# Turning round the column order of every product with weights in a two-layer fp32 encoder

## What is computed

```python
def reference(x, mem, ...):
    h = x
    for l in range(DEPTH):                      # DEPTH = 2
        h = h + hybrid_mixer(rms_norm(h, mix_norm_g[l]), w_in[l], ..., w_out[l])
        h = h + memory_cross_attention(rms_norm(h, xattn_norm_g[l]),
                                       rms_norm(mem, mem_norm_g[l]),
                                       w_xq[l], w_xk[l], w_xv[l], w_xo[l])
        h = h + conv_ffn(rms_norm(h, ffn_norm_g[l]), w_up[l], ffn_conv_w[l],
                         ffn_conv_b[l], w_down[l])
    return rms_norm(h, final_norm_g)
```

## Time and profile before

| | |
|---|---|
| median of 3 runs | 904.4 us (902.22 to 905.19) |
| profiled execution, its own time | 903.87 us |
| span, first to last instruction | 902.0 us |
| mean granted TensorE clock | 0.992 |
| TensorE busy | 879.2 us, 97% |
| VectorE, ScalarE busy | 627.5 and 525.9 us, 70% and 58% |
| moved | 146.7 MB at 163 GB/s |

### The profile page before, as it was taken

One profiled execution on the slowest core, in us unless ns is written; L12 is line 12 of the kernel. 1 busy time (PEld: TensorE's weight loads), 2 busy tenths in 40 slices (PEclk: granted clock), 3 DMA queues, 4 the chain that ended last, 5 costly groups with the idle time before them and its releaser, 6 DMA issues.

```text
span 902.0 us, 13410 instructions
## 1 busy us (share of the span) xinstructions
PE 879.2 (97%) x5452; PEld 774.5 (86%) x5452; DVE 627.5 (70%) x914; ACT 525.9 (58%) x782; POOL 12.9 (1%) x37
## 2 busy tenths in 40 slices
PE   6999999999999999999999999899999899999997
PEld 6999998788888888888899999888888788888885
DVE  5788487858557767667676875877664677667665
ACT  6864573557547556555667546636646555556555
POOL 5000000000000000000000000000000000000000
PEclk9999999999999999999999999999999999999999
DMA  9735543455154655565558254335362356555541
GB/s 284 220 98 158 168 152 131 141 186 187 47 187 155 218 190 184 187 191 183 140 170 225 63 166 159 140 96 187 109 217 94 108 176 230 187 190 184 187 164 47
DMA packets 128679, 146.68 MB, mean 163 GB/s; under 512 B 23164, under 2 KB 109546, under 8 KB 128618
## 3 DMA queue, kind: packets, MB, share of 16 engines
q1 hardware_dynamic: 128404, 145.55, 49.8%
q10 hardware_dynamic: 214, 0.28, 0.1%
HBM read 144.77 MB, written 1.05 MB: 162 GB/s over the span
## 4 chain that ended last, share of the span: by engine, by line
PE 90%; DVE 5%; ACT 4%; issue 1%; DMA 0%; DVEq 0%; ACTq 0%
PE bank L718 21%; PE bank L680 15%; PE bank L682 14%; PE bank L681 14%; PE bank L719 11%; PE bank L753 2%; DVE wlo L1446 2%; PE bank L851 2%; ACT whi L1100 2%; PE bank L1022 2%; PE bank L1009 2%; PE bank L772 1%; PE bank L883 1%; PE bank L893 1%; PE bank L860 1%; PE bank L976 1%
## 5 line engine op out<-in xcount | busy, mean ns | idle before, releaser
L1446 DVE TENSOR_TENSOR wlo<-raw,whi 128x2048 fp32r<-128x2048 f32 (+3 forms) x144 | 306.5, 2134 | 104.9 <-ACT whi L1100 104.4
L718 PE MATMUL bank<-ypair,whi 128*128 128x512 f32 x832 | 294.9, 398 | 0.6 <-DVE ypair L1462 0.5
L1100 ACT ACTIVATE whi<-raw 128x2048 fp32r<-128x2048 f32 (+3 forms) x144 | 256.4, 1786 | 39.5 <-PE bank L682 32.1
L719 PE MATMUL bank<-ypair,wlo 128*128 128x256 f32 x832 | 233.5, 281 | 0.0
L718 PEld LDWEIGHTS bank<-ypair,whi 128*128 128x128 f32 x832 | 156.2, 188 | 40.3 <-DVE wlo L1446 1.4
L719 PEld LDWEIGHTS bank<-ypair,wlo 128*128 128x128 f32 x832 | 157.1, 189 | 0.8
L680 PE MATMUL bank<-xhi,whi 128*128 128x256 f32 x320 | 94.9, 297 | 1.9 <-DVE wlo L1446 1.2
L681 PE MATMUL bank<-xlo,whi 128*128 128x256 f32 x320 | 92.4, 289 | 0.0
L682 PE MATMUL bank<-xhi,wlo 128*128 128x256 f32 x320 | 92.2, 288 | 0.0
L680 PE MATMUL bank<-whi,xhi 128*128 128x512 f32 (+2 forms) x256 | 90.0, 352 | 0.0
L682 PE MATMUL bank<-whi,xlo 128*128 128x512 f32 (+2 forms) x256 | 88.5, 346 | 0.0
(11 more groups left out here) (259 smaller groups left out, 1192.7 us busy)
## 6 DMA issues: line engine op xcount, KB each, us to landing
raw<-in_w_up SPq DMA_DIRECT2D x44, 1024.0 KB, 5.0
raw<-in_w_down SPq DMA_DIRECT2D x22, 1024.0 KB, 4.9
raw<-in_w_in SPq DMA_DIRECT2D x10, 1024.0 KB, 6.1
raw<-in_w_xk SPq DMA_DIRECT2D x8, 1024.0 KB, 4.8
raw<-in_w_xv SPq DMA_DIRECT2D x8, 1024.0 KB, 5.0
raw<-in_w_out SPq DMA_DIRECT2D x8, 1024.0 KB, 5.0
raw<-in_w_xq SPq DMA_DIRECT2D x8, 1024.0 KB, 4.7
raw<-in_w_xo SPq DMA_DIRECT2D x8, 1024.0 KB, 4.9
```

The source lines that it names most:

```text
L718: mm(o, hi[:, k, cs], ypair[:, k].rearrange("p a n -> p (a n)"), start=k == 0, stop=False, skip_group_check=True)
L719: last = mm(o[:, 0:T], lo[:, k, cs], yhi[:, k, :], start=False, stop=k == KT - 1, skip_group_check=True)
L1100: A(whi[:, gu % RING, 0:SIZE[gu]], raw[:, gu % RING, 0:SIZE[gu]], ACT.Copy).then_inc(hi_done, 1)
L1446: tt(wlo[:, gu % RING, 0:n_], raw[:, gu % RING, 0:n_], whi[:, gu % RING, 0:n_], ALU.subtract).then_inc(lo_done, 1)
```

## The change

A new helper `falling` issues every product with weights. It puts `[:, ::-1]` on the output and on the moving operand, so that column n of the output is still the product with moving column n, but the last column goes first. The stationary operand, the counts, the flags and the semaphores stay. For the 512-column product of `fm_joint` the order is that of hi and lo together: the lo half from its last column, then the hi half. The instructions on every engine stand in the same sequence before and after; in the changed kernel all products with weights carry the line of the helper, 681.

```diff
--- before.py
+++ after.py
@@ -676,10 +676,14 @@
                 def have(key):
                     pe.wait_ge(lo_done, UNIT[key] + 1)
 
+                def falling(o, s, m, first, last):
+
+                    return mm(o[:, ::-1], s, m[:, ::-1], start=first, stop=last, skip_group_check=True)
+
                 def split_mm(o, s_hi, s_lo, m_hi, m_lo, first, last):
-                    mm(o, s_hi, m_hi, start=first, stop=False, skip_group_check=True)
-                    mm(o, s_hi, m_lo, start=False, stop=False, skip_group_check=True)
-                    return mm(o, s_lo, m_hi, start=False, stop=last, skip_group_check=True)
+                    falling(o, s_hi, m_hi, first, False)
+                    falling(o, s_hi, m_lo, False, False)
+                    return falling(o, s_lo, m_hi, False, last)
 
                 def weights(key, nk):
                     gu = UNIT[key]
@@ -715,8 +719,8 @@
                             if fresh and f == 0:
                                 lo_is(pe, l, "n2" if name[:2] == "xq" else "n3", k)
                             cs = slice(f * P, f * P + P)
-                            mm(o, hi[:, k, cs], ypair[:, k].rearrange("p a n -> p (a n)"), start=k == 0, stop=False, skip_group_check=True)
-                            last = mm(o[:, 0:T], lo[:, k, cs], yhi[:, k, :], start=False, stop=k == KT - 1, skip_group_check=True)
+                            falling(o, hi[:, k, cs], ypair[:, k].rearrange("p a n -> p (a n)"), k == 0, False)
+                            last = falling(o[:, 0:T], lo[:, k, cs], yhi[:, k, :], False, k == KT - 1)
                         last.then_inc(te_done, 1)
 
                 def fm_unit(name, group, fresh=False):
@@ -750,8 +754,7 @@
                             lo_is(pe, l, group, k)
                         for i, (x, w) in enumerate(((xh, hi), (xh, lo), (xl, hi))):
                             for t in range(TT):
-                                last = mm(bank(names[t])[:, 0:n], x[:, k, t * P:(t + 1) * P], w[:, k, :],
-                                          start=k + i == 0, stop=False, skip_group_check=True)
+                                last = falling(bank(names[t])[:, 0:n], x[:, k, t * P:(t + 1) * P], w[:, k, :], k + i == 0, False)
                     last.then_inc(te_done, 1)
 
                 def tm_unit(unit, names, n, group, fresh=False):
```

## The result

The changed kernel takes 908.7 us in the median of 5 runs (908.19 to 910.38) against 904.4 before (902.22 to 905.19). The ratio is 1.0054, with a 95% interval from 1.0041 to 1.0068: slower by 4.9 us (3.7 to 6.1). The forecast was 904 and no change, with 901 to 907 around it; 908.7 lies outside that, but inside the wide range of 861 to 960, in which both a gain and a loss had a place.

What follows compares the result with a forecast made beforehand. TensorE, busy 97% of the span, was taken to set the end. The profiled 903.87 us + 1,640,448 columns x 0 + 4304 products x 0 gave 903.9, forecast as 904 us, own range 901 to 907, wide range 861 to 960.

Steps and rivals of the forecast that it cites:

- What bounds the kernel: Whole span: TensorE, busy 97%, sets the end; an added nanosecond per product is added to the time in full.
- No instruction moves, the waits stay, the distance between two writes of a column: All engines: counts, flags and waits unchanged; in the joint pair's bank the rewrite distances swap order, costing nothing new.
- The write with a step of minus one: Output of products with weights to PSUM, written backwards: taken as nothing per column, bounded with the read at 0.413 ns.
- The read with that step: Moving operand of products with weights, read backwards from SBUF: taken as nothing per column, slow end 0.413 ns more.
- 4304 x 0: Fixed part of all 4304 products with weights: no change, bounded by 10 ns less and 13 ns more each.
- the zero for each column: The 1,640,448 columns of products with weights: 0 ns more each, as every row with a backward step shows none.
- The prediction's own sign of being wrong: Distances between TensorE starts, 227 ns at 512 columns and 120 at 256: forecast wrong if either moves over 1 ns.
- The nearest rows: VectorE scans, 680 ns either way, and ScalarE and VectorE PSUM reads: a step of minus one is free there.
- Half pace: Rival at every column of products with weights: 0.413 ns more each, + 678 us, 1582 us in all; chance 0.18.
- The start price per product: Rival on 4304 products: a backward pattern costs 0 to 13 ns once each, 0 to 56 us; chance 0.10.
- A smaller fixed part: Rival on 4304 products: the 13 ns shrink to 3 ns, 43 us less, 861 us; chance 0.05.
- the prediction's second reading: Skill's PSUM line rule read as two accesses in a row must share a line: the backward step is free.

Runs made afterwards that it cites:

- The stream kernel: Not the encoder: 32 products a line from one stationary and one moving buffer, no other engine at work; falling against rising, bf16 216 and 216 ns at 512 columns.

## Why the prediction was wrong

**What bounds the kernel** held. TensorE has no cover, and the 5.2 us of the distances are 4.9 in the result. One reading was off: the first 45 us and the last 12 hold 14.8 of TensorE's 22.8 idle us, not all; another 5.9 lie between 560 and 735 us, a window that the rows did not show. They did not matter here.

**No instruction moves, the waits stay, the distance between two writes of a column**: nothing in the runs contradicts them beyond small things. TensorE's wait for `wlo` grew from 1.2 to 2.6 us, and its first wait shrank from 9.5 to 9.0. The joint pair's 353.2 ns fall only 0.4 behind.

**The write with a step of minus one**, taken as free: right, 0.9995.

**The read with that step**: here the sum failed. I had split a product into 0.418 ns a column and a fixed 13 ns from two distances, and taken both as constants of the engine, the second with the reason that the same stationary load stands between the products. The fixed part is not fixed. With a falling read it is 12 ns at 256 columns and 20 at 512. With a rising one it changes with the size of the stationary load (with half of it, from 13 to 7 ns at 256 columns and from 13 to 17 at 512) and with what ran before: the same rising down projection at 227.1 and 229.3 ns, the same joint pair at 346.9 and 352.8. The term that was 4304 x 0 should have been 1104 x 4 to 6.4 ns, 192 x 4 ns and 1056 x -1.7 ns, or 1.2 ns a product in the mean: 5.2 us. Split as the prediction did it, the falling distances would give 0.449 ns a column and 3.5 ns fixed, so the zero for each column failed with it; but that split misses the widths between (175.9 ns for 384 columns, where 177.8 were measured). The prediction's own sign of being wrong, a distance that moves by more than 1 ns, was met at both widths.

**The nearest rows**, scans and PSUM reads backwards on VectorE and ScalarE, were the wrong witnesses. I had written that they have a slower stream and drew the value from them all the same. The stream kernel shows the limit: TensorE itself is as indifferent as they are with bf16 and plain float32.

**The rivals.** Half pace did not happen: at 512 columns 438 ns were named and 233 came. The start price per product (chance 0.10, 0 to 56 us) had the sign and the size in its range, but the wrong law; it was to be the same at 256 and at 512 columns, and it is a loss at one and a gain at the other. A smaller fixed part (0.05) came true for 256 columns alone.

**The rule on lines** in the Trainium skill, page "SBUF — State Buffer", section "Door 1: The DMA port swizzle", sets the limit for SBUF at 16-byte lines and names PSUM as the place where a pattern costs. For PSUM the runs bear out the prediction's second reading, by which a fall is free: turned round it costs nothing (0.9995). For SBUF the rule does not give what was measured: blocks of 4 float32r columns that fall, each as long as a line and read in full, cost as much as a plain fall (233.4 ns), while a fall inside blocks of 4 costs nothing (226.6).

**Still open**: by what the read's order, the stationary load and the preceding stream set the 227, 229 or 233 ns of a product; what puts the pairs on the faster pace where nothing falls; and where the gain of the 256-column products goes.

## What to carry to other kernels

Where TensorE sets the end, measure the distance between starts, not the duration, and for each width: a change of half a per cent can be the sum of a loss at one width and a gain at another. An effect of a few nanoseconds a product need not add up over parts of a change, since a stream's pace can depend on what entered it; here three turned products ahead of each 32 pairs saved 3.8 us, nearly as much as the whole change had cost. Take the price of a new access from the engine and the data type that will make it, or keep the range open.

## What the runs showed of the hardware that was not expected

- With 128 stationary columns a float32r product reads its moving columns in order at 227 ns for 512 and 120 for 256; from last to first at 233 and 118; bf16 takes 216 at 512 in both directions. With 64 stationary columns it is 230 and 114 in order, 233 and 118 backwards. Writing PSUM backwards is free (0.9995).
- Blocks of 16 columns that rise, read backwards inside, cost 266.6 ns at 512 columns, 18% more than in order; blocks of 64 falling cost 227.5.
- A repeated pair of a 512- and a 256-column product has two steady paces, 352.8 and 346.9 ns, and keeps the one it entered for 32 pairs. Falling products ahead of it can put it on the faster one, and it is also found there without any.
